# Differential attention layer on one core: the second product on the top left block joined to 512 columns

## The reference

```
proj = u @ w_in                       # 512x2048 @ 2048x8192 -> q | k | v | z
lam = exp(sum(lam_q1*lam_k1)) - exp(sum(lam_q2*lam_k2)) + lam_init
logits = q_blk @ k.T * scale + relative position bias, causal mask   # 16 heads of 128
p = softmax(logits); a = p[:, :, 0] - lam * p[:, :, 1]               # 8 pairs of heads
o = rms_norm(a @ v, subln_g) * (1 - lam_init)                        # v: 256 wide for a pair
y = (o * silu(z)) @ w_out             # 512x2048 @ 2048x2048
out = layer_norm(alpha * x + y, ln_g, ln_b)
```

## Time and profile before

| | us |
|---|---|
| median of 3 runs | 876.25 (876.14 to 876.38) |
| the profiled execution | 876.08 |
| its span in the trace | 874.3 |
| PE busy | 866.6 (99%) |
| PE weight loads | 769.4 (88%) |
| DVE busy | 710.1 (81%) |
| ACT busy | 454.6 (52%) |
| POOL busy | 281.4 (32%) |

### The profile page before, as it was taken

One profiled execution on the slowest core, in us unless ns is written; L12 is line 12 of the kernel. 1 busy time (PEld: TensorE's weight loads), 2 busy tenths in 40 slices (PEclk: granted clock), 3 DMA queues, 4 the chain that ended last, 5 costly groups with the idle time before them and its releaser, 6 DMA issues.

```text
span 874.3 us, 14306 instructions
## 1 busy us (share of the span) xinstructions
PE 866.6 (99%) x5050; PEld 769.4 (88%) x5050; DVE 710.1 (81%) x1072; ACT 454.6 (52%) x695; POOL 281.4 (32%) x496
## 2 busy tenths in 40 slices
PE   9999999999999999999999999999999999999997
PEld 8888899999999999999989898989898978888886
DVE  5686778897888788878988898889788986976986
ACT  4445555545555555555555554555556563655511
POOL 1301516151606150525152515251424215130033
PEclk9999999999999999999999999999999999999999
DMA  8822685777587677757685768576857765997733
GB/s 298 317 84 80 143 221 117 218 177 201 116 241 168 184 149 237 151 174 162 226 159 172 166 219 163 171 167 192 172 151 176 275 225 145 231 180 245 273 123 115
DMA packets 54092, 161.38 MB, mean 185 GB/s; under 512 B 9760, under 2 KB 11808, under 8 KB 53808
## 3 DMA queue, kind: packets, MB, share of 16 engines
q0 software_dynamic: 24928, 71.37, 40.2%
q1 hardware_dynamic: 24720, 80.49, 25.8%
q10 hardware_dynamic: 4416, 9.18, 3.1%
HBM read 143.66 MB, written 13.15 MB: 179 GB/s over the span
## 4 chain that ended last, share of the span: by engine, by line
PE 96%; DVE 2%; DMA 0%; issue 0%; ACT 0%; SPq 0%; DVEq 0%; ACTq 0%
PE proj L1760 50%; PE att L1760 46%; DMA w_raw<-w_in_tiles_dram 0%; DVE w_split L1182 0%; DVE w_split L1166 0%; DVE scratch L1342 0%; DVE big L1752 0%; DVE scratch L1369 0%; ACT scratch L907 0%; DVE scratch L1325 0%; DVE last_stats L1738 0%; DVE operands L1320 0%; DVE x_res L1226 0%; DVE xg_split L1489 0%; DVE proj L1263 0%
## 5 line engine op out<-in xcount | busy, mean ns | idle before, releaser
L801 ACT ACTIVATE w_split<-w_raw 128x1024 fp32r<-128x1024 f32 x196 | 206.9, 1059 | 157.0 <-PE proj L1760 85.7
L1166 DVE TENSOR_TENSOR w_split<-w_raw,w_split 128x1024 fp32r<-128x1024 f32 x196 | 238.2, 1218 | 52.0 <-ACT w_split L801 51.0
L1760 PE MATMUL att<-w_split,xg_split 128*128 128x512 f32 (+1 forms) x832 | 170.8, 361 | 0.0
L1760 PEld LDWEIGHTS att<-w_split,xg_split 128*128 128x128 f32 x832 | 142.4, 189 | 24.3
L691 POOL DMA_DIRECT2D scratch<-scratch x256 | 127.7, 593 | 41.8 <-DVE scratch L1369 32.4
L1760 PE MATMUL proj<-w_split,xg_split 128*128 128x256 f32 (+1 forms) x800 | 137.4, 330 | 1.4 <-DVE operands L1320 0.7
L1760 PEld LDWEIGHTS proj<-w_split,xg_split 128*128 128x128 f32 x800 | 120.5, 190 | 15.8 <-DVE operands L1320 1.2
L1760 PE MATMUL proj<-xg_split,w_split 128*128 128x256 f32 (+1 forms) x752 | 126.4, 327 | 0.3 <-DVE w_split L1509 0.3
L1760 PEld LDWEIGHTS proj<-xg_split,w_split 128*128 128x128 f32 x752 | 112.0, 191 | 12.8 <-issue 0.6
L714 POOL DMA_DIRECT2D w_raw<-w_in_tiles_dram x84 | 73.9, 889 | 130.3 <-DVE w_split L1166 101.5
L1760 PE MATMUL proj<-w_split,sums 128*128 128x256 f32 (+1 forms) x656 | 103.5, 317 | 0.0
(11 more groups left out here) (191 smaller groups left out, 1020.6 us busy)
## 6 DMA issues: line engine op xcount, KB each, us to landing
w_raw<-w_in_tiles_dram SPq DMA_DIRECT2D x98, 512.0 KB, 4.2
w_raw<-w_in_tiles_dram POOLq DMA_DIRECT2D x84, 512.0 KB, 5.8
w_raw<-w_out_tiles_dram SPq DMA_DIRECT2D x19, 512.0 KB, 3.7
w_raw<-w_out_tiles_dram POOLq DMA_DIRECT2D x12, 512.0 KB, 8.1
bias_by_distance<-bias_lines POOLq DMA_DIRECT2D x8, 640.0 KB, 6.1
scratch<-scratch POOLq DMA_DIRECT2D x128, 40.0 KB, 2.8
bias<-bias_by_distance POOLq DMA_DIRECT2D x8, 512.0 KB, 4.1
scratch<-scratch POOLq DMA_DIRECT2D x128, 32.0 KB, 2.0
```

What stands on the lines that cost most here:

```text
L801: nc.scalar.activation(split_view(a, 0), pair_raw(a), ACT.Copy).then_inc(w_hi, 1)
L1166: nc.vector.tensor_tensor(split_view(a, 1), pair_raw(a), split_view(a, 0).bitcast(F32), ALU.subtract).then_inc(w_ready, 1)
L1760: return nc.tensor.matmul(dst, lhsT, rhs, start=start, stop=stop, skip_group_check=True)
```

## The change

Step 6 becomes wide: `wide_banks` gives it both halves of the banks of `half_banks(h, 0)`, and it is taken into `WIDE`. It no longer opens its accumulation the narrow way. `finish_lower` then has three adds: the first half of the banks onto `kept_first`, then the second half plus `kept_first` into region 6, then the add for region 5 as before. The second waits for the first and the third for the second, because the third writes the half of the banks that the second reads.

```
         def wide_banks(h, step):
-            if step in (0, 3):
+            if step in (0, 3, 6):
                 return half_banks(h, 0)
...
                 dve.wait_ge(lower_begun, phase_number(p, h) + 1)
                 dve.wait_ge(quarter_done, slots_before(p) + (h + 1) * PHASE)
-                nc.vector.tensor_tensor(region_of(h, 6), region_of(h, 6), kept_first, ALU.add).then_inc(upper_left_done, 1)
+                halves = wide_banks(h, 6)
+                nc.vector.tensor_tensor(kept_first, halves[:, :, 0], kept_first, ALU.add).then_inc(upper_left_begun, 1)
+                dve.wait_ge(upper_left_begun, phase_number(p, h) + 1)
+                nc.vector.tensor_tensor(region_of(h, 6), halves[:, :, 1], kept_first, ALU.add).then_inc(upper_left_done, 1)
+                dve.wait_ge(upper_left_done, phase_number(p, h) + 1)
                 nc.vector.tensor_tensor(region_of(h, 5), wide_banks(h, 5)[:, :, 1], kept_sum, ALU.add).then_inc(lower_done, 1)
...
-                opens = c == 0 and step in (4, 6)
+                opens = c == 0 and step == 4
...
-WIDE = {0: None, 1: 2, 2: 0, 3: None, 5: 0}
+WIDE = {0: None, 1: 2, 2: 0, 3: None, 5: 0, 6: None}
```

More of the change, by code:

```diff
@@ L268, in diff_layer @@
         sum_begun = sem("sum_begun")
+        upper_left_begun = sem("upper_left_begun")
         upper_left_done = sem("upper_left_done")
```

## The result

The changed kernel takes 877.63 us in the median of 20 runs (875.99 to 879.63), the kernel before 876.19 (875.54 to 879.03). The ratio is 1.0016, with a 95% interval of 1.0009 to 1.0022: slower by 1.4 us, where 1.25 us less was forecast. The profiled execution has a span of 875.9 us against 874.3.

The account below looks back on a forecast made before the run. TensorE was taken to bound the inner pairs, VectorE a stretch of the last: -13 x 0.16 + 0.84 = -1.24 us from 876.08 gives 874.84, adjusted by 0.17 to 875.0; range 874.5 to 875.5, 74 in 100.

Parts of the forecast that it names:

- The saving: Step 6 in each half pair: fewer, wider matmuls over the same columns take 0.16 us less on TensorE.
- The price of the third add: Each half pair's end on VectorE: three dependent adds take 2.12 us instead of 1.28, so 0.84 us more.
- The last wait: Last pair's end, before the output projection's third row tile: 0.84 us added in full, last 0.16 saving lost, idle about 1.7.
- I cost the 13 half pair ends before the last at nothing: All half pair ends but the last: the added 0.84 us on VectorE is hidden by cover and costs 0.
- the splits for slots 17 and 3: VectorE's weight splits behind the adds, ending 5.2 and 3.0 us before TensorE reaches those slots: cover for the 0.84.
- at most 0.84 us later, several slots ahead of their use: POOL's accumulating transfers wait for VectorE's weight sums; this small delay was claimed harmless.
- The gap at 369.12: VectorE idle 1.08 us waiting for ACT, which follows TensorE; taken as a sign that lateness does not pile up.
- The signs of being wrong: Last-pair idle time stays at 0.74 us, pieces of 64 matmuls exceed 11.25 us, or VectorE enters an inner pair's chain.
- the third one: Inner pairs: the prediction is wrong if their chain of waits has VectorE in it; no size given.
- the chain from 679.71 to 702.31: Last pair, scores' end to TensorE's return: the chain was read as VectorE with one ACT step, at 700.98.
- VectorE becomes the bound: Slot 3 split at pair ends: 0.84 us at 14 ends less the saving, 9.5 slower, 885.8; 6 in 100.

Follow-up runs that it names:

- the wide step alone: Changed kernel without the third add, the high times low half of step 6's result left out: 874.19 us, ratio 0.9977 to the kernel before.
- plain transfers: Changed kernel with the 84 accumulating input weight transfers as plain ones, the block sum left out: 874.97 us; the kernel before with the same: 876.30 us.
- third add alone: Kernel before, TensorE's work unchanged, with a third dependent add of the same size at each half pair's end, result unused: 879.12 us, ratio 1.0030.

## Why the prediction was wrong

- **The saving** of 0.16 us for a half pair: right (11.17 to 11.21 for 11.35; the wide step alone gains 2.07 us).
- **The price of the third add**, 0.84 us: right (0.72 + 0.73 us to the third start; from the end of the scores to TensorE's return 23.72 us in place of 22.86).
- **The last wait is not hidden, the last saving lost**: right, by the trace of the changed kernel and of the one with plain transfers, both 1.6 us.
- **"I cost the 13 half pair ends before the last at nothing": this step failed**, and with it the sign. The sum is -2.08 + 0.84 plus some 2.6 us (877.63 against 875.0). It failed in two places. First, I priced the cover of the work behind the adds (the splits for slots 17 and 3, 5.2 and 3.0 us) and not the thinnest cover on the same engine: the z halves, 0.38 us ahead of each next pair. They stand ahead of that half pair's own adds and so looked untouched; the lateness comes to them from the adds before. Second, "at most 0.84 us later, several slots ahead of their use" on POOL's transfers: in the kernel before, ScalarE already stood idle for 2.18 us for one of them (249.77), and in the changed kernel it was issued 0.15 us later, the two before it 1.0 us later, and it landed 1.44 us later. The run with plain transfers, in which the loss is gone, says the same. The gap at 369.12 that I took for slack does end with TensorE, as I read it (ScalarE's split at 368.02 had waited for TensorE's `att`); but it is one gap of many, and I read it for all. In the kernel before ScalarE's weight splits waited for landings 14 times, 23.7 us in all, beside 100 times for TensorE.
- **The signs of being wrong**: the third one came, the chain of an inner pair has VectorE in it. One reading was incomplete without bearing on the sum: the chain from 679.71 to 702.31 has a second ACT step, 1.32 us at 681.00.
- **The rival "VectorE becomes the bound"** had the sign, and neither place nor price: it asked for lags above 3.0 us ahead of slot 3 and gave 885.8.
- Shown: the add is the cause (third add alone, wide step alone), and the accumulating transfers are the link (plain ones restore 874.97, and change nothing in the kernel before). The way from half 0's add to the stall at 268.72 can be followed in the traces above, through a later weight sum, a later landing and later splits. Only argued: the way to the other stalls, and why four of the six inner pair ends lose nothing. Half 1's add outside the last pair costs 1.1 us, and the one stall seen with it stands ahead of the scores; whether it comes there through the turning of the gated result on POOL (the chain of the changed kernel around 226 to 238 runs so) was not tried by itself.

## What to carry to other kernels

Before an operation is added to an engine that works in order, list every wait of the bounding engine on it with its cover, not the one behind the new operation alone; the thinnest counts, also where it stands half a loop away. Idle time pays lateness back only where what ends it does not depend on the late engine, so follow each idle gap to its source: here it was a transfer that the late engine itself had released. And when a small gain is eaten, putting the thinly covered work earlier in the order can be better than giving the gain up (874.26 us here, with both the z operations and the last pair's end moved; the z operations alone gave 876.49).

## What the runs showed of the hardware

Transfers from POOL that accumulate landed in 5.8 us in the median, the same transfers without accumulation in 3.9, with the same 512 KB and the same queue. The time to land moves with the issues before it: for one place of the program it was 9.4 us in the kernel before and 10.7 in the changed one, with the third of three issues 0.15 us later and the other two 1.0 us later.

The changed kernel spread over 3.6 us in 20 runs and 4.6 in 12 (875.97 to 880.53), the same program with plain transfers over 0.75 us in 11. Accumulation alone does not make this spread: the wide step alone has the same transfers and 22 waits of ScalarE for them, and its 11 runs spread over 1.7 us.
